# A two-block float32 network on one core: modulation and time steps computed on 32-column strips, attention row scores spread over eight key tiles

## The reference, cut to what matters

```python
silu_c = silu(c); silu_cc = silu(c_ctx)                       # two vectors of 1024
sh_a, sc_a, g_a, sh_f, sc_f, g_f = split(silu_c @ w_mod + b_mod, 6)   # w_mod: 1024 x 6144
hc = ctx * (1 + mod_c[1]) + mod_c[0]                          # mod_c: silu_cc @ w_mod + b_mod
hx = x * (1 + sc_a) + sh_a
dt = softplus(dt_raw + dt_bias)                               # dt_raw: 32 columns of h @ w_in, per token
s  = q @ k.T * scale                                          # 16 heads of 64, 1280 keys, 1024 queries
pr = softmax(s); o = pr @ v
```

## Time and profile before

| what | us |
|---|---|
| median of 3 runs | 4129.87 (4126.40 to 4130.62) |
| the profiled execution, its own time | 4116.66 |
| its span, first to last instruction | 4114.9 |
| mean granted clock of TensorE | 0.913 of 2.4 GHz |
| TensorE matmuls busy | 3523.0 (86%) |
| VectorE, ScalarE, GpSimd busy | 1342.5, 541.1, 567.3 |

### The profile page before, as it was taken

One profiled execution on the slowest core, in us unless ns is written; L12 is line 12 of the kernel. 1 busy time (PEld: TensorE's weight loads), 2 busy tenths in 40 slices (PEclk: granted clock), 3 DMA queues, 4 the chain that ended last, 5 costly groups with the idle time before them and its releaser, 6 DMA issues.

```text
span 4114.9 us, 28731 instructions
## 1 busy us (share of the span) xinstructions
PE 3523.0 (86%) x10980; PEld 1763.6 (43%) x10980; DVE 1342.5 (33%) x2183; ACT 541.1 (13%) x1022; POOL 567.3 (14%) x592
## 2 busy tenths in 40 slices
PE   7986776967679999999994999739688999999997
PEld 7544343433367333333442444325544444444443
DVE  1333765032322454553223332262612021112113
ACT  0111111110000222222011111131211000000001
POOL 0000222000000555555001000030800000000000
PEclk9996887988866999999996999959789999999998
DMA  6000001010026000001005889820001001000101
GB/s 247 22 23 0 0 1 62 11 41 21 0 102 247 14 1 1 1 1 33 28 13 187 287 310 334 301 78 0 31 21 62 21 31 61 31 31 31 61 10 46
DMA packets 170597, 288.09 MB, mean 70 GB/s; under 512 B 22216, under 2 KB 108912, under 8 KB 169968
## 3 DMA queue, kind: packets, MB, share of 16 engines
q1 hardware_dynamic: 155632, 237.02, 16.8%
q10 hardware_dynamic: 10240, 32.71, 2.1%
q0 software_dynamic: 4608, 16.78, 1.1%
HBM read 236.17 MB, written 50.33 MB: 70 GB/s over the span
## 4 chain that ended last, share of the span: by engine, by line
PE 64%; issue 12%; DVE 10%; POOL 7%; DMA 4%; ACT 2%; SPq 0%; ACTq 0%; POOLq 0%; DVEq 0%
PE ps L1509 15%; PE ps L1523 7%; PE ps L1207 5%; PE ps L840 5%; PE ps L390 5%; PE ps L1669 4%; PE ps L321 4%; POOL arena_b L1083 4%; PE ps L739 3%; PE ps L2605 3%; DMA ring<-in_w_up 3%; PE ps L1688 2%; PE ps L1933 1%; PE ps L1951 1%; PE ps L650 1%
## 5 line engine op out<-in xcount | busy, mean ns | idle before, releaser
L1509 PE MATMUL ps<-arena_a,ring 128*128 128x512 f32 x1408 | 607.7, 593 | 1.3 <-DVE arena_a L1890 1.3
L1509 PEld LDWEIGHTS ps<-arena_a,ring 128*128 128x128 f32 x1408 | 268.0, 190 | 338.9 <-issue 337.4
L1083 POOL TENSOR_TENSOR arena_b<-arena_b 128x512 f32<-128x512 f32 x288 | 357.8, 1267 | 392.3 <-ACT arena_b L1065 390.2
L1523 PE MATMUL ps<-ring,arena_d 128*128 128x512 f32 x704 | 303.8, 592 | 0.0
L1101 DVE TENSOR_REDUCE arena_b<-ps 128x1 f32<-128x512 f32 (+1 forms) x384 | 213.0, 597 | 260.2 <-PE ps L985 253.7
L985 PE MATMUL ps<-arena_d,arena_a 64*128 64x512 f32 (+1 forms) x768 | 247.1, 566 | 21.3 <-DVE arena_b L1101 19.1
L840 PE MATMUL ps<-ring,arena_b 128*128 128x512 f32 x384 | 194.2, 669 | 82.7 <-DVE arena_c L922 51.4
L1669 PE MATMUL ps<-ring,arena_a 128*128 128x512 f32 x496 | 233.5, 626 | 31.5 <-issue 14.9
L1007 PE MATMUL ps<-arena_a,arena_d 64*128 64x512 f32 x640 | 238.2, 627 | 0.5 <-DVE arena_b L1121 0.5
L1065 ACT ACTIVATE arena_b<-ps 128x512 f32<-128x512 f32 x320 | 173.7, 594 | 440.4 <-PE ps L1011 440.4
L1557 DVE TENSOR_TENSOR arena_d<-arena_t,ps 128x512 f32<-128x512 f32 x44 | 30.2, 687 | 582.3 <-ACT arena_t L1547 582.3
(11 more groups left out here) (445 smaller groups left out, 3841.2 us busy)
## 6 DMA issues: line engine op xcount, KB each, us to landing
ring<-in_w_gate SPq DMA_DIRECT2D x42, 1024.0 KB, 7.5
ring<-in_w_up SPq DMA_DIRECT2D x42, 1024.0 KB, 10.0
ring<-in_w_down SPq DMA_DIRECT2D x42, 1024.0 KB, 5.5
ring<-in_w_mod SPq DMA_DIRECT2D x12, 2048.0 KB, 8.1
ring<-in_w_in SPq DMA_DIRECT2D x10, 2048.0 KB, 8.6
xslots<-arena_c SPq DMA_DIRECT2D x1, 15872.0 KB, 48.0
arena_a<-xslots ACTq DMA_DIRECT2D x31, 512.0 KB, 5.5
yslots<-arena_a ACTq DMA_DIRECT2D x31, 512.0 KB, 5.4
```

The lines of the kernel that those rows point to most:

```text
L1083: eng.tensor_tensor(acc, first, prT[n % NPR], ALU.add).then_inc(s_pa, 1)
L1509: mm = eng.matmul(ps[:, 2 * (u % 2) + w, :], guw[s][:, k, w * FE + f * P:w * FE + (f + 1) * P], hT[:, k, half * HALF:(half + 1) * HALF], s ...
L1523: mm = eng.matmul(ps[:, 4 + m % 4, :], hid[s][:, f, t * P:(t + 1) * P], dnw[s][:, f, h * HALF:(h + 1) * HALF], start=(f == 0), stop=(f == 1))
```

## The change

Four edits. (1) Modulation: the stationary operand is now the condition vectors, padded with zeros to 32 columns (`csp`), and the moving one a 512-column row block of the panel. The 8 blocks k of a panel go to four column strips of the array (i = k % 4, PSUM partitions 32i to 32i+31), two on each. VectorE copies the 128 x 512 partial sums to SBUF (`mpart`), and four matmuls of 2 columns with a selection matrix `sel` add the four strips and turn them to column form. The panel is released after its 8 matmuls. (2) Time steps: the same with `wdtw` stationary and the tokens moving, in pieces of 512, 512 and 256; one VectorE copy of 1280 columns; ten matmuls with `sel`. (3) Attention: row scores of the next job are spread over eight key tiles, `split` and `shifts` stand at tile 7 of VectorE's program, `turn_shifts` at tile 9. (4) GpSimd builds `sel` at the start; `sgn` moves from a tensor of its own to a column of `convw`; semaphore counts are shifted (left out below).

```diff
+        sel = sb("sel", [P, 32])
...
+            eng.memset(sel[:, :], 0.0).then_inc(s_const, 1)
...
+            for i in range(4):
+                eng.affine_select(out=sel[:, :], in_=sel[:, :], compare_op=ALU.not_equal, fill=1.0,
+                                  base=-32 * i, pattern=[[-1, 32]], channel_multiplier=1).then_inc(s_const, 1)
+                eng.wait_ge(s_const, 12 + i + 1)
...
-            eng.wait_ge(s_const, 11)
+            eng.wait_ge(s_const, 16)
...
-        def pe_mod(eng, part, j0, n0, n1):
-
+        csp = [view(arena_c, 1024, KT, 32), view(arena_t, 0, KT, 32)]
+        mpart = [[view(arena_c, at + i * HALF, HALF) for i in range(2)] for at in (0, 9216)]
+        MODN = (4, 8)
+        MOD_SET, MOD_COPIED = (0, 6 + 6 + 1), (2, 6 + 6 + 3)
+        MOD_SUMS = (1, 8)
+
+        def dve_condition(eng, part):
+            step(eng, eng.memset(csp[part], 0.0), s_rawz, MOD_SET[part] + 1)
             eng.wait_ge(s_silu, 1)
-            for j in range(n0 // 4, n1 // 4):
-                wait_panel(eng, j0 + j - n0 // 4)
-                w = slot(j0 + j - n0 // 4)
-                for b in range(4):
+            eng.tensor_copy(csp[part][:, :, 0:2], csil[:, :, :]).then_inc(s_rawz, 1)
+
+        def pe_mod(eng, part, j0, n0):
+            n = MODN[part]
+            eng.wait_ge(s_rawz, MOD_SET[part] + 2)
+            for j in range(n + 1):
+                if j < n:
+                    wait_panel(eng, j0 + j)
+                    w = slot(j0 + j)
+                    if j >= 2:
+                        eng.wait_ge(s_rawz, MOD_COPIED[part] + j - 1)
                     for k in range(KT):
-                        mm = eng.matmul(ps[:, part, 2 * (4 * j + b):2 * (4 * j + b) + 2],
-                                        w[:, k, b * P:(b + 1) * P], csil[:, k, :],
-                                        start=(k == 0), stop=(k == KT - 1))
-                mm.then_inc(s_mod, 1)
+                        i = k % 4
+                        mm = eng.matmul(ps[32 * i:32 * i + 32, 2 + j % 2, :], csp[part][:, k, :], w[:, k, :],
+                                        start=(k < 4), stop=(k >= 4))
+                    mm.then_inc(s_mod, 1)
+                if j >= 1:
+                    eng.wait_ge(s_rawz, MOD_COPIED[part] + j)
+                    for b in range(4):
+                        at = 2 * (n0 + 4 * (j - 1) + b)
+                        mm = eng.matmul(ps[:, part, at:at + 2], mpart[part][(j - 1) % 2][:, b * P:(b + 1) * P],
+                                        sel[:, 0:2], start=True, stop=True)
+                    mm.then_inc(s_packT, 1)
 
         def dve_mod(eng, part, n0, n1):
-            eng.wait_ge(s_mod, n1 // 4)
+            dve_condition(eng, part)
+            for j in range(MODN[part]):
+                eng.wait_ge(s_mod, 4 * part + j + 1)
+                if j >= 2:
+                    eng.wait_ge(s_packT, MOD_SUMS[part] + j - 1)
+                eng.tensor_copy(mpart[part][j % 2], ps[:, 2 + j % 2, :]).then_inc(s_rawz, 1)
+            eng.wait_ge(s_packT, MOD_SUMS[part] + MODN[part])
...
+            for b, src in enumerate((hx[:, :, 0:HALF], hx[:, :, HALF:L], hc)):
+                for k in range(KT):
+                    i = k % 4
+                    mm = eng.matmul(ps[32 * i:32 * i + 32, b, 0:src.shape[2]], wdtw[:, k, :], src[:, k, :],
+                                    start=(k < 4), stop=(k >= 4))
+            mm.then_inc(s_packT, 1)
+            eng.wait_ge(s_rawz, 6 + 6 + 1)
             for t in range(NT):
-                for k in range(KT):
-                    mm = eng.matmul(ps[:, 0, t * 32:(t + 1) * 32], h_tile(k, t), wdtw[:, k, :],
-                                    start=(k == 0), stop=(k == KT - 1))
+                mm = eng.matmul(ps[:, 0, t * 32:(t + 1) * 32], dtp[:, t * P:(t + 1) * P], sel[:, :],
+                                start=True, stop=True)
             mm.then_inc(s_packT, 1)
...
-            eng.wait_ge(s_packT, 1 + 1)
+            eng.wait_ge(s_packT, 6)
+            eng.tensor_copy(dtp, ps[:, 0:3, :].rearrange("p a n -> p (a n)")[:, 0:L + CTX]).then_inc(s_rawz, 1)
+            eng.wait_ge(s_packT, 7)
...
-        EARLY = (2, 2, 2, 2, 2, 2, 0, 0, 0, 0)
+        EARLY = (2, 1, 2, 1, 2, 1, 2, 1, 0, 0)
...
-                    if kt == 7 and j + 1 < NJOB:
+                    if kt == NT - 1 and j + 1 < NJOB:
                         turn_shifts(j + 1)
...
-                    if kt == 5 and j + 1 < NJOB:
+                    if kt == 7 and j + 1 < NJOB:
                         split(j + 1)
                         shifts(j + 1)
...
-        sgn = sb("sgn", [P, 1])
+        sgn = convw[:, 0:1]
```

More of the change, by code:

```diff
@@ L238, in build @@
         s_dta = sem("dt_act_steps")
-        s_xbc, s_rawz, s_raw, s_conv = sem("xbc_product"), sem("raw_zeroed"), sem("raw_copied"), sem("convolved")
+        s_xbc, s_rawz, s_raw, s_conv = sem("xbc_product"), sem("partials_copied_and_raw_zeroed"), sem("raw_copied"), sem("convolved")
         s_act = sem("conv_activated")
@@ L286, in pool_consts @@
                 eng.memset(m[:, :], 1.0).then_inc(s_const, 1)
-            eng.wait_ge(s_const, 6)
+            eng.memset(sel[:, :], 0.0).then_inc(s_const, 1)
+            eng.wait_ge(s_const, 7)
             eng.affine_select(out=identz[:, :], in_=identz[:, :], compare_op=ALU.not_equal, fill=1.0,
@@ L452, in act_xbc @@
             after(eng, "hx")
-            eng.wait_ge(s_rawz, 6)
+            eng.wait_ge(s_rawz, 6 + 6)
             for m in range(XT + 1):
@@ L476, in build @@
         ends["xbc"] = [(s_xbc, XT), (s_act, XT), (s_xsc, 3 * (XT - 2)), (s_xsT, 3 * (XT - 2)), (s_conv, XT)]
+        dtp = view(arena_a, 0, L + CTX)
         def pe_dt(eng):
@@ L510, in dve_dt @@
             ch(eng.tensor_tensor(dta, dts, bc(eacs[:, 0, :], 1, NT), ALU.mult))
-            eng.wait_ge(s_packT, 2 + 1)
+            eng.wait_ge(s_packT, 8)
             fw = ps[:, 1, 0:NT * 16].rearrange("p (t h) -> p t h", h=16)
@@ L940, in pe_mod2 @@
             after(eng, "qkv")
-            pe_mod(eng, 1, J_MOD, 16, MODT)
+            pe_mod(eng, 1, J_MOD, 16)
         def dve_mod2(eng):
@@ L1363, in pool_places @@
             eng.iota(sloti, [[1, NSLOT]], base=0, channel_multiplier=0).then_inc(s_const, 1)
-            eng.wait_ge(s_const, 16 + N_TABLES - 1)
+            eng.wait_ge(s_const, 21 + N_TABLES - 1)
             eng.tensor_copy(slotno, sloti).then_inc(s_const, 1)
         def sp_zero(eng):
-            eng.wait_ge(s_const, 16 + 1)
+            eng.wait_ge(s_const, 21 + 1)
             eng.dma_start(xslots.rearrange("(s p) d -> p s d", p=P), bc(zeros, 1, NSLOT)).then_inc(s_spill, 16)
@@ L1375, in dve_router @@
             ch = Chain(eng, s_rt)
-            eng.wait_ge(s_packT, 3 + 1)
+            eng.wait_ge(s_packT, 16 + 1)
             def first_of(oh, v, mx):
@@ L1407, in dve_router @@
             place = Chain(eng, s_place)
-            eng.wait_ge(s_const, 16 + N_TABLES)
+            eng.wait_ge(s_const, 21 + N_TABLES)
             for e16, oh in ((exp1, oh1), (exp2, oh2)):
@@ L1418, in dve_router @@
             ch(eng.tensor_tensor(w2, w1, ew, ALU.mult))
-            eng.wait_ge(s_packT, 3 + 2)
+            eng.wait_ge(s_packT, 16 + 2)
             place(eng.tensor_copy(pfx[0][:, 4:, :], ps[:, 2, 0:P].rearrange("p (t e) -> p t e", e=NE)))
@@ L2049, in pool_s5_consts @@
             eng.memset(jrot[:, :], 0.0).then_inc(s_const, 1)
-            eng.wait_ge(s_const, 11 + 2)
+            eng.wait_ge(s_const, 16 + 2)
             eng.affine_select(out=sgn[:, :], in_=sgn[:, :], compare_op=ALU.is_ge, fill=-1.0,
                               base=SP2 - 1, pattern=[[0, 1]], channel_multiplier=-1).then_inc(s_const, 1)
-            eng.wait_ge(s_const, 11 + 3)
+            eng.wait_ge(s_const, 16 + 3)
             for base, fill in ((-SP2, -1.0), (SP2, 1.0)):
@@ L2058, in pool_s5_consts @@
                                   base=base, pattern=[[-1, P]], channel_multiplier=1).then_inc(s_const, 1)
-                eng.wait_ge(s_const, 11 + (4 if fill < 0 else 5))
+                eng.wait_ge(s_const, 16 + (4 if fill < 0 else 5))
         def sp_s5_params(eng):
@@ L2113, in dve_s5_params @@
             eng.wait_ge(s_5t, 1)
-            eng.wait_ge(s_const, 11 + 5)
+            eng.wait_ge(s_const, 16 + 5)
             eng.wait_ge(s_5a, 1)
@@ L2727, in _ @@
             pe_pack(eng)
-            pe_mod(eng, 0, 0, 0, 16)
+            pe_mod(eng, 0, 0, 0)
             pe_hx(eng)
```

## The result

The changed kernel takes **3972.76 us** (median of 3 runs, 3969.19 to 3977.30) against 4129.87: a ratio of 0.9622 with the 95% interval 0.9601 to 0.9644. The profiled executions stand at 4116.66 and 3972.76, so 143.9 us between them where the sum said 141.

What follows compares the result with a forecast made beforehand. TensorE, busy 86% of the span, was taken as the bound. Savings of 29.4 + 70.5 + 20.3 + 21 = 141 us from the 4129.9 median gave 3989 us, own range 3976 to 4000, wide range 3968 to 4018.

Steps and rivals of the forecast that it cites:

- the sum: Savings in both modulation parts, time steps and attention together: 29.4 + 70.5 + 20.3 + 21 = 141 us.
- The main step: Modulation and time steps: a pass costs its instruction and weights, 0.214 us, not columns; four strips run at once.
- The forecast on the median: Whole kernel: 4129.9 - 141 = 3989 us, from the median of the kernel before.
- Part 0: Modulation part 0: the fourth panel's landing sets the end, 47 us against 76.4: -29.4 (bounds -28 and -31.5).
- Part 1: Modulation part 1: panel loads become the bound; it ends at 1223.3 us against 1293.8: -70.5.
- Time steps: Time-step matmuls, copy and sums take 14 us against 34.3: -20.3 (bounds -19 and -25).
- so I don't lean on it: Sums in modulation: a pass might cost half of 0.214 us if pace follows the clock; the forecast kept 0.214.
- Attention: Attention: a job takes 38.2 us against 39.6; fifteen jobs give -21 (bounds 0 and -35).
- The Trainium skill's figure: Column-strip matmuls: at 3.07 times for four strips a panel takes 2.2 or 4.5 us, the sum some 4 us smaller.
- Rival D: Modulation and time steps: strips take turns at 1.2 GHz, each pass awaiting its load; slower, 4214 us; chance 0.02.

Runs made afterwards that it cites:

- the repeat: The changed kernel once more, nothing edited, beside the kernel before: 3973.95 us against 4118.3, ratio 0.9638.
- e2: The changed kernel with the old time steps (80 matmuls, 32 columns moving): 4000.31 us, ratio 0.9698 to the kernel before.

## Why the prediction was right

The main step, that the passes were paid by instruction and not by column, and that a panel belongs on four strips as the moving operand, held: the undone parts, the one-strip and the two-strip run bear it out. The sum is closer than its parts: 141 for 143.9, with misses of 1.2 to 3.9 us both ways that cancel. The forecast on the median was 16 us too high, since it took over the 13 us by which the median of the kernel before stood above its trace; beside the repeat that median is 4118.3. By its terms:

- **Part 0** -27.8 for -29.4: the last panel came when forecast. Behind it stood 3.64 + 3.50 us, the upper end of the range (7.0) and not the 5.7 taken. TensorE had waited 9.5 us and was at 1.2 GHz. In the repeat the sums ran at 2.4 GHz again (1.98 us), and part 0 ended at 46.6, so this miss is within what the clock varies by from run to run.
- **Part 1** -69.3 for -70.5. The new bound is the loads, and the last panel what is late; with the strips halved the stage lengthens by only 1.7.
- **Time steps** -22.9 for -20.3. Matmuls 7.43 for 8, copy 1.50 for 1.3 to 1.7, but sums 2.43 for 4.3. This is the term that was most mis-sized: "so I don't lean on it" kept the 0.214 us for a pass, and the timeline shows 0.12 at 2.4 GHz. The clock of 1.00 beside part 0 in the earlier trace rows misled: the pace there was that of 1.2 GHz. Right behind it, with the column still at 1.00, eight passes of one form take 1.74 us to the next instruction and a little later 0.88, in TensorE's timeline of the kernel before:

```profile
76.23 1.95 PE L354 MATMUL ps<-ident,arena_a 128*128 128x128 f32 x8
77.97 0.63 PE L354 MATMUL ps<-ident,arena_d 128*128 128x128 f32 x2
...
82.40 1.04 PE L354 MATMUL ps<-ident,arena_a 128*128 128x128 f32 x8
```

  So for the first 80 us the column can't be taken at its word; the pace of a form seen at both levels can.
- **Attention** -23.0 for -21. The job is 0.25 shorter than forecast: a single pair costs 0.42 (2.72 less 2.30), not 0.53, which takes 0.44 off the four single intervals, and tile 8 gives 0.2 back. Over the fifteen jobs that is 24.3 us (589.8 against 565.5); 1.3 were lost ahead of the first product with V. Both kernels begin attention at 1.2 GHz, and the changed one stays there longer (mean granted clock 0.55 over 1176 to 1181 us, against 0.93 over 1300 to 1305 before).
- **Outside the terms**: the scan came 3.9 us shorter and the experts 3.7 longer; the two cancel here, by luck, and neither was foreseen. The experts' difference is within their variation. The scan's is only in part: both traces with the old time steps have it at 340.1 us (the kernel before and e2), the twelve with the new ones at 335.9 to 338.9. So 1.2 to 4.2 us seem to go with that edit. TensorE's mean granted clock in the scan's first 40 us is 0.65 in the two and 0.67 to 0.71 in the twelve; that this is the reason was not isolated.
- **The Trainium skill's figure** of 3.07, weighed ahead of the run, would have made the gain some 4 us smaller by that estimate. The panel took 1.92 and not 2.2, as L1021 had it in the earlier trace rows.

Rival D (strips in turn at 1.2 GHz, each behind its own load) had no trace: even one strip on its own takes 6.99 us a panel at 2.4 GHz, 0.44 a pass.

## What to carry to other kernels

When a matmul has one narrow operand, see which side it stands on. If 128 x 128 blocks of the wide one are loaded for a few moving columns, the price is the block's (here 0.12 or 0.214 us a pass, by the clock); make the narrow one stationary in 32 columns and stream the wide one on four column strips. Then ask at once for the load that is late next: here two strips gave nearly all of it. And a pair of instructions on two halves of the array is worth keeping in step: put work that waits for nothing between two pairs that share a slower reader, and keep that reader's long instructions (a reciprocal) out of their reach.

## What the runs showed of the hardware

- **Small VectorE steps beside GpSimd.** The changed kernel splits its maxima at tile 7, while GpSimd adds. VectorE's timeline, then GpSimd's:

```profile
1339.58 0.18 DVE L1152 TENSOR_REDUCE arena_b<-arena_b 128x8 f32<-128x24 f32 x1
1339.79 0.36 DVE L1153 CAST arena_b<-arena_b 128x8 bf16<-128x8 f32 x1
1340.18 0.17 DVE L1154 TENSOR_TENSOR arena_b<-arena_b 128x8 f32<-128x8 f32 x1
1340.39 0.19 DVE L1155 CAST arena_b<-arena_b 128x8 bf16<-128x8 f32 x1
1340.62 1.22 DVE L1156 TENSOR_TENSOR arena_b<-arena_b 128x8 f32<-128x8 f32 x1
1341.86 1.21 DVE L1157 CAST arena_b<-arena_b 128x8 bf16<-128x8 f32 x1
```

```profile
1337.62 2.49 POOL L1125 TENSOR_TENSOR arena_b<-arena_b 128x512 f32<-128x512 f32 x2 [2.36 <-ACT arena_b L1107]
1340.54 4.93 POOL L1125 TENSOR_TENSOR arena_b<-arena_b 128x512 f32<-128x512 f32 x4 [0.43 <-ACT arena_b L1107]
```

  While GpSimd is idle (1340.11 to 1340.54) the steps take 0.17 and 0.19 us. The same kinds of step take 1.2 once it adds again, about one GpSimd addition (4.93/4 = 1.23), and the cast that begins at 1339.79 beside the earlier additions takes 0.36 and ends at 1340.15, right behind them. The Trainium skill, "SBUF — State Buffer", section "Who interferes with whom", describes such a lock: VectorE and GpSimd share a port pair, one holds it for its whole instruction and the other is fully blocked. It says that casts can contend, and two-input operations with both inputs in SBUF beside a GpSimd instruction that reads SBUF, which the two stretched lines are, and that on trn2 reductions never do. The trace agrees: L1152 runs beside GpSimd's additions in 15 jobs and is at 0.18 in each. That this lock is the cause is argued from the trace, not isolated by a run. The prediction gave these steps no price; with the turn at tile 9 the tile in between covers them, and with the turn one tile earlier the stage is 44 us longer.
- **Two row halves out of step** cost 1.04 us a double: 5.04 against 4.00 with the pair split.
- **Column strips** are nearly free of each other: 1.97 times with two, 3.76 with four (512 columns, float32, 2.4 GHz).
- **A pass of 2 columns with 128 x 128 weights** takes 0.12 us at 2.4 GHz and 0.214 to 0.224 at 1.2 GHz, and with 32 columns 0.12 and 0.214. So the old loops, in which TensorE had no gap for 54 and 109 us, ran at about twice the price that a clock at its upper level would have given them. Whether anything else would have raised it was not tried.
- **A reciprocal** of 512 columns out of PSUM takes 3.36 us, five times the 0.69 of a reduction or a multiplication of as many.
